# One encoder layer on 8 cores: every operation of the merged stage is issued one step behind the operation that feeds it

## The reference

```python
def _layer(x, ...):
    p = x @ w_in                                   # columns q | k | v | u | gate_b | gate_c, 512 each
    attn = _mixed_dilated_attention(q, k, v)       # 8 heads of 64
    conv = gate_b * conv3_centred(gate_c * u)      # depthwise, width 3
    mix = concat(rms(attn) * g_attn, rms(conv) * g_conv) @ w_o
    x = layernorm(ALPHA * x + mix)
    return layernorm(ALPHA * x + (silu(x @ w_gate) * (x @ w_up)) @ w_down)

# attention: for (window, dilation) in ((128,1), (512,4), (2048,16)): each query sees the keys at
# offsets k*dilation, |k| <= window/(2*dilation), with ALiBi; the three results are combined with
# softmax(lse) over the three configurations
```

## Time and profile before

| what | us |
|---|---|
| median of three runs | 4218.82 |
| the three runs | 4218.82, 4288.22, 3841.24 |
| profiled execution | 3844.42 |
| its span on the slowest core (core 2) | 3842.9 |
| spans of the 8 cores | 3789.4 to 3842.9 |
| PE, DVE, ACT, POOL busy in the span | 3283.0, 1625.3, 1096.0, 1568.6 |
| merged stage, up to its last matmul | about 1615 |
| first matmul of the second stage | 1659.5 |

### The profile page before, as it was taken

The page is one execution under the profiler, slowest core; times in us unless marked ns, Lnnn a source line. Parts: engine busy times, 40 slices in busy tenths (PEclk is TensorE's granted clock), DMA queues, the critical chain, the costliest instruction groups (busy, mean ns, idle before and its releaser), DMA issues.

```text
span 3842.9 us, 55077 instructions; the slowest of 8 cores (3789.4 to 3842.9 us)
## 1 busy us (share of the span) xinstructions
PE 3283.0 (85%) x18570; PEld 1555.6 (40%) x18570; DVE 1625.3 (42%) x2292; ACT 1096.0 (29%) x1355; POOL 1568.6 (41%) x1059
## 2 busy tenths in 40 slices
PE   5896777687677777559999999999999999999998
PEld 2342334343333333324444444444444444444443
DVE  1222554555555655524334343433433343344332
ACT  0112545665554454411111111111111111111110
POOL 1343553343336776533334244333424433442432
PEclk8998888888878888869999999999999999999999
DMA  8546447685554443353432433343243324333422
GB/s 143 147 106 125 127 115 164 145 190 135 143 142 119 126 108 100 75 167 104 154 121 94 153 131 122 104 154 121 95 153 137 122 99 159 126 103 133 148 99 72
DMA packets 309857, 488.13 MB, mean 127 GB/s; under 512 B 168304, under 2 KB 229872, under 8 KB 302320
## 3 DMA queue, kind: packets, MB, share of 16 engines
q1 hardware_dynamic: 291712, 396.52, 33.1%
q0 software_dynamic: 17872, 88.09, 11.0%
HBM read 440.49 MB, written 110.10 MB: 143 GB/s over the span
## 4 chain that ended last, share of the span: by engine, by line
PE 68%; DMA 12%; ACT 6%; DVE 5%; issue 4%; POOL 3%; SPq 2%; DVEq 0%; ACTq 0%; POOLq 0%
PE psc L674 50%; PE psa L289 17%; DMA a_Vt<-vs 3%; DVE a_At L570 2%; DMA c_wr<-wgu 2%; ACT a_rec L567 2%; DMA qs<-a_st 2%; DMA ks<-a_st 1%; SPq L257 1%; ACT a_rec L566 1%; DMA a_win<-wgu 1%; DMA a_st<-w_o 1%; POOL a_ct L347 1%; DVE a_acc L555 1%; ACT a_rec L568 1%
## 5 line engine op out<-in xcount | busy, mean ns | idle before, releaser
L289 PE MATMUL psa<-a_xT,a_win 128*128 128x512 bf16 (+1 forms) x2816 | 686.7, 396 | 131.0 <-DVE a_st L286 44.8
L521 POOL TENSOR_TENSOR a_PT<-a_PT,a_et 128x1024 bf16<-128x1024 bf16 x192 | 414.0, 2158 | 593.9 <-ACT a_PT L518 592.5
L674 PE MATMUL psc<-c_x1T,c_wr 128*128 128x512 bf16 x2816 | 629.7, 380 | 23.8 <-DMA c_wr<-wgu 13.7
L674 PE MATMUL psc<-c_x1T,a_win 128*128 128x512 bf16 x2816 | 631.3, 381 | 17.3 <-ACT c_x1T L759 10.2
L776 DVE TENSOR_TENSOR c_hT<-psc,c_sg 128x512 bf16<-128x512 f32 x352 | 243.5, 692 | 875.9 <-PE psc L674 818.5
L775 ACT ACTIVATE c_sg<-psc 128x512 f32<-128x512 f32 x352 | 210.2, 597 | 1138.2 <-PE psc L674 1125.6
L518 ACT ACTIVATE a_PT<-psa 128x1024 bf16<-128x1024 f32 x384 | 385.8, 1022 | 257.6 <-PE psa L289 247.9
L289 PEld LDWEIGHTS psa<-a_xT,a_win 128*128 128x128 bf16 x2816 | 271.9, 103 | 461.0 <-issue 216.1
L702 POOL TENSOR_TENSOR c_sc<-c_sc,c_mhalf 128x1 f32<-128x1 f32 x128 | 78.9, 616 | 839.6 <-DVE c_sc L701 839.1
L674 PEld LDWEIGHTS psc<-c_x1T,c_wr 128*128 128x128 bf16 x2816 | 274.6, 98 | 357.4 <-issue 32.3
L674 PEld LDWEIGHTS psc<-c_x1T,a_win 128*128 128x128 bf16 x2816 | 275.1, 98 | 351.9 <-issue 26.9
(11 more groups left out here) (77 smaller groups left out, 3266.5 us busy)
## 6 DMA issues: line engine op xcount, KB each, us to landing
a_win<-wgu SPq DMA_DIRECT2D x176, 512.0 KB, 3.4
c_wr<-wgu SPq DMA_DIRECT2D x176, 512.0 KB, 3.5
c_x<-xo SPq DMA_DIRECT2D x64, 512.0 KB, 8.4
yo<-c_ob POOLq DMA_DIRECT2D x64, 512.0 KB, 3.0
a_Vt<-vs SPq DMA_DIRECT2D x128, 240.0 KB, 5.3
a_xT<-xt POOLq DMA_DIRECT2D x28, 1024.0 KB, 10.2
a_Vt<-vs SPq DMA_DIRECT2D x128, 192.0 KB, 4.1
qs<-a_st SPq DMA_DIRECT2D x128, 128.0 KB, 2.9
```

The source lines that it names most:

```text
L289: op("tensor", lambda e: e.matmul(out, lhsT=lhsT, rhs=rhs, start=start, stop=stop, skip_group_check=True), reads=reads, writes=[PS(b)])
L521: op("vector" if g % 2 else "gpsimd", lambda e: e.tensor_tensor(out=pv4, in0=pv4, in1=tab, op=ALU.mult), reads=["et"], writes=[("PT", psl)])
L674: P.op("tensor", lambda e: e.matmul(out, lhsT=lhsT, rhs=rhs, start=start, stop=stop), reads=reads, writes=writes)
```

## The change

- `tick` runs after the matmuls of each projection and issues what `defer` has put off: the evacuation of a projection comes after the matmuls of the next one, its store one projection after that; so do the `gcs` copy, the `hb` product, `conv_pool` (a projection after `hb`) and the products and stores of `gate_b`.
- `front(g)` only issues the scores. `exps(g - 1)` and `mults(g - 2)` follow in the same step, and `back` of a pair comes at the even step g for g - 4 and g - 3 (before: at the odd g for g - 3 and g - 2). V tiles are loaded after `back` and no longer before the scores.
- `norm` has two `rec` buffers and the order ACT chunk 0, ACT chunk 1, DVE 0, DVE 1, ACT 2, ACT 3, DVE 2, DVE 3, then two empty places and the store; two of these are popped at the start of a step. They are no longer flushed before `acc` is written.
- `avail` is raised 4 projections later; `zero_fill` is in four parts, after tiles 2 to 5; the DVE product of `wo_load` comes 6 projections after its DMA.
- The identity comes by a casting DMA from POOL's queue, ahead of w_in, and not by SP and a DVE cast.

```diff
+            def defer(n, fn):
+                late.append([n, fn])
+
+            def tick():
+                for it_ in late:
+                    it_[0] -= 1
+                while True:
+                    due = [it_ for it_ in late if it_[0] <= 0]
+                    if not due:
+                        break
+                    late.remove(due[0])
+                    due[0][1]()
+
             def mm(out, lhsT, rhs, start, stop, reads, b):
...
                 b = proj(0 if kind == "q" else 1, j, xs)
-                ss = cnt["st"] % NST
-                cnt["st"] += 1
-                evac(st[ss], bank(b), b, [("st", ss)])
...
+                def fin():
+                    ss = cnt["st"] % NST
                     cnt["st"] += 1
-                    evac(st[s2].rearrange("p (r i) -> p r i", r=16), bank(b).rearrange("p (i r) -> p r i", r=16), b, [("st", s2)])
-                    load("sync", qs2[j, :, g0:g0 + 512], st[s2], [("st", s2)], [("qs2", c, n, j)], "st%d" % s2)
+                    evac(st[ss], bank(b), b, [("st", ss)])
+                    if kind == "q":
+                        dst, key = qs[j, :, g0:g0 + 512], ("qs", c, n, j)
+                    else:
+                        dst, key = ks[j, :, c * WIN + n * 512: c * WIN + (n + 1) * 512], ("ks", c, n, j)
+                    defer(1, lambda: load("sync", dst, st[ss], [("st", ss)], [key], "st%d" % ss))
+                    if kind == "q":
+                        s2 = cnt["st"] % NST
+                        cnt["st"] += 1
+                        evac(st[s2].rearrange("p (r i) -> p r i", r=16), bank(b).rearrange("p (i r) -> p r i", r=16), b, [("st", s2)])
+                        defer(1, lambda: load("sync", qs2[j, :, g0:g0 + 512], st[s2], [("st", s2)], [("qs2", c, n, j)], "st%d" % s2))
...
-                    for _ in gate_u(j, xs, hb[hs][:, j, 2:514], [("hb", hs, j)]):
+                    for _ in gate_u(j, xs, hb[hs][:, j, 2:514], [("hb", hs, j)], then=(lambda j: lambda: conv_pool(hs, j))(j)):
                         yield
-                    conv_pool(hs, j)
...
-                    if i == 1:
-                        zero_fill()
+                    if 1 <= i <= 4:
+                        zero_fill(i - 1)
...
-                        avail[0] += 1
+                        defer(4, more)
+
+            def more():
+                avail[0] += 1
 
             def wo_load(j):
                 load("sync", wos, w_o_d[j * 128:(j + 1) * 128, :], [], [("st", q) for q in range(4)], "c_wo")
-                op("vector", lambda e: e.tensor_scalar(out=wo[:, j, :], in0=wos, scalar1=gct[:, j:j + 1], scalar2=None, op0=ALU.mult), reads=[("st", q) for q in range(4)] + ["gct"], writes=[("win", 0), ("win", 1)])
-
-            def zero_fill():
+                defer(6, lambda: op("vector", lambda e: e.tensor_scalar(out=wo[:, j, :], in0=wos, scalar1=gct[:, j:j + 1], scalar2=None, op0=ALU.mult), reads=[("st", q) for q in range(4)] + ["gct"], writes=[("win", 0), ("win", 1)]))
...
-            def zero_fill():
+            def zero_fill(k):
                 zb = acc[:].rearrange("p h n -> p (h n)").bitcast(BF16)
-                for side in range(2):
-                    t = side * (WIN - HALO)
+                side = k % 2
+                t = side * (WIN - HALO)
+                if k < 2:
...
+                else:
...
+            def exps(g):
+                psl, sp = g % NPT, g % 2
                 op("scalar", lambda e: e.activation(out=PT[psl][:], in_=pp[sp][:], func=AF.Exp, scale=0.125), writes=[PS(2 * sp), PS(2 * sp + 1), ("PT", psl)])
+
+            def mults(g):
+                ui, blk, _, di, m = bank_info(2 * g)
+                hp, psl = units[ui][2], g % NPT
...
-                        while norm_q:
-                            norm_q.pop(0)()
+                        assert norm_done[0] >= 4 * ui + (m + 1 if ui else 0) - (4 if ui else 0)
...
+                def chunk_act(m):
+                    cs, rc = slice(512 * m, 512 * m + 512), rec[m % 2]
...
+                def chunk_dve(m):
+                    cs, rc = slice(512 * m, 512 * m + 512), rec[m % 2]
...
+                A, B, nop = chunk_act, chunk_dve, lambda: None
+                seq = [(A, 0), (A, 1), (B, 0), (B, 1), (A, 2), (A, 3), (B, 2), (B, 3)]
+                for fn, m in seq:
+                    norm_q.append((lambda fn, m: lambda: fn(m))(fn, m))
+                norm_q.extend([nop, nop, store])
...
+                if g < NG and not ready(g // 24):
+                    return False
+                for _ in range(2):
+                    if norm_q:
+                        norm_q.pop(0)()
                 if g < NG:
-                    if not ready(g // 24):
-                        return False
                     want_kq = g // 24 + (1 if g % 24 >= 4 else 0)
                     while state["kq"] <= want_kq and ready(state["kq"]):
                         kq_load(state["kq"])
                         state["kq"] += 1
-                    if g % 2 == 0:
-                        while state["v"] <= g // 2 + 2 and ready(state["v"] // 12):
-                            v_load(state["v"])
-                            state["v"] += 1
                     front(g)
-                if g >= 3 and g % 2 == 1:
+                if 1 <= g <= NG:
+                    exps(g - 1)
+                if 2 <= g <= NG + 1:
+                    mults(g - 2)
+                if g % 2 == 0 and g >= 4:
+                    back(g - 4)
                     back(g - 3)
-                    back(g - 2)
-                for _ in range(2):
-                    if norm_q:
-                        norm_q.pop(0)()
+                if g % 2 == 0 and g < NG:
+                    while state["v"] <= g // 2 + 2 and ready(state["v"] // 12):
+                        v_load(state["v"])
+                        state["v"] += 1
                 state["i"] += 1
...
+            while late:
+                tick()
```

## The result

The changed kernel takes 3741.9 us in the median of four runs, the profiled one 3742.37. Against the kernel before (3841 and 3844 us on that chip) the ratio is **0.9736, 95% interval 0.9708 to 0.9765**: 2.6% faster, some 100 us, where 3675 us, 170 less, was forecast. The runs at 4191, 4219 and 4288 us, in which a die ran slower, are left out of it. On a second chip the same kernel gave 0.9766 (0.9745 to 0.9787).

The account below looks back on a forecast made before the run. Before 1660 us no engine is full; TensorE's waits on other engines bound the merged stage. Terms 60 + 21 + 14 + 11 + 36 + 28 = 170 us off 3844 gave 3675 us, range 3580 to 3800.

Parts of the forecast that it names:

- V tiles: TensorE's waits for V loads in the merged stage: claimed to keep their 45 us, so no gain.
- clock: Matmuls at the lower clock in the merged stage: a third of the 85 us comes back, 28 us.
- order waits: Exponentials, multiplies and evacuations standing behind the next TensorE work: 36 us gained, between -10 and 60.
- normalisation: Largest term, at fifteen unit ends: two rec buffers cut TensorE's wait from 12.6 to 8.6 us each, 60 us.
- zero fills: Ten DMAs on SP after the second tile: split up, they end a 14.19 us wait; gain 14 us, at least 8.
- first K: Start of attention: release four projections later lets SP catch up, halving a 22.23 us wait; gain 11 us, between 0 and 15.
- POOL's part of the order waits: TensorE's waits for POOL's table products: half of their 33.1 us goes, as convolutions no longer precede urgent multiplies.
- w_o product: DVE's product behind its DMA in wo_load: six projections later its data has landed; four waits go, 21 us.
- DVE's part of the order waits: DVE's small waits (multiply, add, yst and gsave writes): about as much again as half of POOL's 33.1 us.
- The chain only moves: Rival: normalisation waits stay as long in more pieces, order waits return as others; 3798 us, chance 0.20 (3767 to 3920).
- Banks come back late: Rival: deferred evacuations return projections' two PSUM banks late; 3950 us at 1.0 us each, chance 0.08 (above 3920).

Follow-up runs that it names:

- e5: Kernel before with only the w_o product seven projections behind its DMA and the zero fills in four parts; 0.9947 of the kernel before.
- e15: Changed kernel with each convolution's five POOL instructions issued as 1, 2 and 2 in three successive projections; 0.9681 of the kernel before.
- e7: Changed kernel with the normalisation spread in half chunks, one per attention step over eight steps; 0.9823 of the kernel before.
- e11: Changed kernel with two DVE reciprocals in place of ACT's Ln, Ln, Exp in the normalisation; 1.0485 of the kernel before.
- e6: Kernel before with only the store of a unit's normalised tile At issued six attention steps later; 0.9999 of the kernel before.
- e10: Kernel before with only the PV pair one attention step later and the V load behind it; 0.9931 of the kernel before.
- e12: Kernel before with only the second stage's weight casts issued singly instead of two in a row; 0.9975 of the kernel before.
- e1: Changed kernel with the normalisation as before: one rec buffer, whole chunks, popped at a step's end; 0.9999 of the kernel before.
- e3: Changed kernel with the attention step and normalisation as before, evacuations, stores and the rest still deferred; 1.0139 of the kernel before.
- e2: Changed kernel with evacuations, convolution and stores issued at once, attention still one step late; 1.0175 of the kernel before.
- e13: Changed kernel with K, Q and first V tiles loaded early, single weight casts and the convolution in three pieces; 0.9644 of the kernel before.

## Why the prediction was wrong in size

The direction, the main term's sign and the ends of the range held. That the size came out no further off is luck: without the 41 us at the V tiles, which no term had, the gain would have been some 61 us instead of 170. The steps that failed are the clock and the order waits: 64 us of the forecast, and together 17 us of loss in the runs. Forecast and found, in us of gain:

| term | forecast | found |
|---|---|---|
| normalisation | 60 | 44 (189 - 145; by the rougher count 63) |
| zero fills | 14 | 14 (waits from 100 to 335 us, 22.8 to 9.3) |
| first K | 11 | -3 |
| POOL's part of the order waits | 17 | -14 |
| w_o product | 21 | 17 (four waits of 20.9 us, one of 4.1 left) |
| DVE's part of the order waits | 19 | -5 (the rest of the 94) |
| barrier | 0 | 8 |
| clock | 28 | 2 (busy time 3283.0 to 3281.2) |
| V tiles | 0 | 41 |

**The clock term** failed in the step "I give back the same third of the 85 us". I had split the gap of 455 us into 360 of waiting and 85 to 95 of slow matmuls, and gave back a third of the latter. The granted clock did rise. The projections' matmuls gave 14 of the 28 us, P·V and scores took 12 of them again, and TensorE's busy time fell by 2. The sum of waits alone accounts for the result. The rule cited from the Trainium skill ("TensorE: Matmul & The Clock Gate", "Loop structure matters more than you think") ties the clock to gaps between bursts. The rise of the granted clock agrees with it; the 85 us that would come back by it did not.

**The w_o product and the zero fills** were sized rightly. DVE's idle time ahead of the product is gone, as said; it brought 17 us here and 19 in e5. The zero fills brought their 14 us here and nothing in e5: the forecast put this gain down to the four parts, and it needs the deferred stores as well.

**Order waits** failed in the sentence "A convolution's five POOL instructions no longer get in front of a multiply that is needed at once". They still do, only a projection later, and POOL's row rose by 14 us. e15 splits the block and brings the row to 19.9 us, near the half of 33.1 that was forecast. DVE's small waits didn't shrink either: those for its table products are 16.4 us where they were 16.7, those for `gsave` 12.6 where they were 11.6.

**First K** failed in "Release four projections later lets SP catch up". SP was held by the `ys` stores, these by DVE, DVE by POOL's convolutions, and four projections are not enough for a chain that advances by 5.0 us where TensorE takes 1.8.

**The normalisation** was sized from ACT's queue alone: 8.6 per unit against 9.6 found, in two pieces of 2.8 to 7.5 us where three of 2.3 to 3.7 were forecast. e7 shows that finer cutting doesn't help; that ACT's work alone sets the waits is argued, and e11 agrees.

**V tiles** are the error in my favour: "so they keep their 45 us of waiting" was wrong. Four trials (e5, e6, e10, e12) left 31 to 43 us of the 45 in the kernel before; e1 and e3, with stores deferred, have 18.0 and 20.9, mostly in one wait each; e2, with attention deferred, has none. So later stores and later attention each seem to take a part, and single casts take 14 us; which share belongs to which stays open. A V wait is only counted where V comes last, so part of it may have been hidden by the longer exponential waits of e2.

**Rivals.** Of "The chain only moves" one half came: the order waits came back under POOL and DVE. The other half did not, the ends got shorter. "Banks come back late" was absent from the changed kernel (TensorE's waits for evacuations, gates and adds fell from 152 to 57 us) and decided e3. I argued against it that everything ahead of an evacuation has its inputs by then. With attention deferred these waits stayed at 57 us; without it, in e3, they were 335.

## What to carry to other kernels

Deferring is a property of a whole queue: the evacuations and stores without attention, or attention without them, were 1.4 to 1.8% slower here, all of them together 2.6% faster. Moving P·V and its load alone (e10) was 0.7% faster, so ask of each move whether something ready comes to stand behind something that isn't. Price what an engine does in one uninterrupted piece (5.7 us of normalisation, 5.8 us of convolution) against what stands behind it, and spread that piece only where the engine has spare time at the finer grain: it paid on POOL and not on ACT. A gain in granted clock counts only if TensorE's busy time falls with it; look at it one shape at a time.

## What the hardware showed beyond expectation

- Reciprocals on DVE of 64x512 float32 took 3.35 us, three times a product of that size (1.03 us) and five times an evacuation of 128x512 (0.69 us). The Trainium skill's "VectorE: DVE Perf Modes", in "Walkthrough: the 8-slice pipeline in each mode", describes it as an iterative divide with a repeat count of 8; the measured time agrees with a slow operation.
- Behind two 512 KB casting DMAs from POOL's queue one DMA issue of SP lasted 17.8 us in the kernel before (17.1 and 15.4 in e5 and e6). With single casts the longest `vs` store issue lasted 9.2 us in e12, and a `ks` one 11.6 in e13. Issues of 8 to 12 us also stand in these traces ahead of the first cast.
- Two instructions of the same size on DVE differ by a factor of nearly three: `At` products took from 1.01 to 2.93 us in the changed kernel, with a median of 1.03 and a mean of 1.47. The Trainium skill's "GPSIMD Engine Reference" (table of specifications) names contention with POOL for DVE instructions with two SBUF inputs, as these have. The trace agrees: the 59 products beside which POOL ran nothing took 1.01 to 1.08 us, and each of the 36 over 1.5 us overlapped with a POOL instruction by about a microsecond or more. DVE's table products took at most 0.69 us without POOL beside them (49 of 192), and up to 3.83 us with it.
